# Experts' outputs as token rows, four of ten output groups held in PSUM, and h kept by rows only

## The reference

```python
def peer(x, w_q, sub_keys, u_tab, v_tab):
    ...
        q = jnp.einsum('td,dc->tc', xb, w_q).reshape(PEER_BLOCK, PEER_HEADS, 2, D_KEY // 2)
        s = jnp.einsum('thcd,hcnd->thcn', q, sub_keys, preferred_element_type=jnp.float32)
        ...
        sc, sel = lax.top_k(cand, PEER_TOPK)
        expert = jnp.take_along_axis(cid, sel, axis=-1)
        g = jax.nn.softmax(sc, axis=-1)
        a = jnp.einsum('td,thkd->thk', xb, u_tab[expert], preferred_element_type=jnp.float32)
        coef = (g * jax.nn.gelu(a, approximate=False)).astype(xb.dtype)
        return jnp.einsum('thk,thkd->td', coef, v_tab[expert])

def channel(h, norm_g, w_q, sub_keys, u_tab, v_tab):
    y = peer(rms_norm(h, norm_g).reshape(B * T, D), w_q, sub_keys, u_tab, v_tab)
    return h + y.reshape(B, T, D)
```

## Time and profile before

| | |
|---|---|
| median of three runs | 3685.9 us (3684.55 to 3686.02) |
| the profiled execution, first to last instruction | 3683.9 us |
| TensorE matmul busy | 3206.2 us, 87% |
| VectorE busy | 2776.0 us, 75% |
| ScalarE busy | 1194.5 us, 32% |
| GpSimd busy | 1217.5 us, 33% |

### The profile page before, as it was taken

One profiled execution on the slowest core, in us unless ns is written; L12 is line 12 of the kernel. 1 busy time (PEld: TensorE's weight loads), 2 busy tenths in 40 slices (PEclk: granted clock), 3 DMA queues, 4 the chain that ended last, 5 costly groups with the idle time before them and its releaser, 6 DMA issues. The chain is left out here.

```text
span 3683.9 us, 63681 instructions
## 1 busy us (share of the span) xinstructions
PE 3206.2 (87%) x22587; PEld 2843.2 (77%) x22587; DVE 2776.0 (75%) x6688; ACT 1194.5 (32%) x2269; POOL 1217.5 (33%) x1214
## 2 busy tenths in 40 slices
PE   7999588999367778647579999999999999999998
PEld 5777355666135556547479999999999999999998
DVE  6553455333124889899679999999999999999998
ACT  5443244444122322259622222222122122222221
POOL 0000122222120000000055565555655565555554
PEclk9999799999678888879889999999999999999999
DMA  4322789887676655307799999999999999999997
GB/s 146 117 66 73 254 275 335 274 297 240 240 265 208 205 194 212 120 26 220 214 365 356 330 343 349 330 348 354 332 344 341 344 348 337 342 348 327 348 342 274
DMA packets 405555, 993.05 MB, mean 270 GB/s; under 512 B 37938, under 2 KB 165908, under 8 KB 404052
## 3 DMA queue, kind: packets, MB, share of 16 engines
q0 software_dynamic: 150048, 595.57, 44.8%
q1 hardware_dynamic: 252932, 383.53, 30.2%
q10 hardware_dynamic: 2368, 11.54, 0.8%
HBM read 911.56 MB, written 146.44 MB: 287 GB/s over the span
## 5 line engine op out<-in xcount | busy, mean ns | idle before, releaser
L2118 PE MATMUL banks<-x_hi,u_hi 128*128 128x320 f32 x2048 | 634.1, 310 | 52.6 <-DVE x_lo L2207 52.6
L2131 PE MATMUL banks<-coef_hi,v_hi 128*128 128x320 f32 x2048 | 633.7, 309 | 6.9 <-issue 6.0
L2118 PE MATMUL banks<-x_lo,u_hi 128*128 128x320 f32 x2048 | 633.9, 310 | 0.0
L2118 PE MATMUL banks<-x_hi,u_lo 128*128 128x320 f32 x2048 | 633.8, 309 | 0.0
L2131 PE MATMUL banks<-coef_lo,v_hi 128*128 128x320 f32 x2048 | 633.5, 309 | 0.0
L2131 PE MATMUL banks<-coef_hi,v_lo 128*128 128x320 f32 x2048 | 633.4, 309 | 0.0
L2079 POOL DMA_INDIRECT uv_row<-in_v_rows,expert_tok x384 | 477.6, 1244 | 385.4 <-DVE y_tok L2261 335.1
L2079 POOL DMA_INDIRECT uv_row<-in_u_rows,expert_tok x384 | 462.9, 1205 | 347.7 <-DVE dots L2235 295.9
L2261 DVE SCALAR_TENSOR_TENSOR y_tok<-uv_row,share,y_tok 128x1024 f32<-128x1024 f32 x415 | 530.3, 1278 | 0.7
L2235 DVE CUSTOM_DVE_ANT_0 uv_row<-uv_row,x_tok 128x1024 f32<-128x1024 f32 x416 | 506.2, 1218 | 0.0
L2118 PEld LDWEIGHTS banks<-x_hi,u_hi 128*128 128x128 f32 x2048 | 385.3, 188 | 52.8 <-DVE x_lo L2207 52.8
(11 more groups left out here) (256 smaller groups left out, 5408.2 us busy)
## 6 DMA issues: line engine op xcount, KB each, us to landing
keys_ps<-in_cache_k SPq DMA_DIRECT2D x256, 256.0 KB, 4.8
values_ps<-in_cache_v POOLq DMA_DIRECT2D x256, 256.0 KB, 4.6
uv_raw<-in_u SPq DMA_DIRECT2D x128, 512.0 KB, 7.5
uv_raw<-in_v SPq DMA_DIRECT2D x128, 512.0 KB, 7.6
scratch_gates<-stage SPq DMA_DIRECT2D x10, 4096.0 KB, 23.6
gates<-scratch_gates SPq DMA_DIRECT2D x128, 320.0 KB, 6.4
out_win_k_out<-in_state_k POOLq DMA_DIRECT2D x8, 4088.0 KB, 15.1
out_win_v_out<-in_state_v POOLq DMA_DIRECT2D x8, 4088.0 KB, 26.5
```

Source lines behind the costliest of these rows:

```text
L2118: ins = nc.tensor.matmul(bank[:, 2 * r + c, 0:CH], u[r][a][:, k * P:(k + 1) * P], x2[b][:, k, c * CH:(c + 1) * CH], start=(k == 0 and a == b),
L2131: ins = nc.tensor.matmul(bank[:, 4 + n % 4, 0:CH], v[j][a][:, k * P:(k + 1) * P], coef[j][b][:, c * CH:(c + 1) * CH], start=(j == 0 and a ...
```

## The change

The outputs are computed with the operands swapped: a 128x128 slice of coef (128 experts by 128 tokens) is stationary and 512 columns of v move, so that the product is 128 tokens by 512 values. There are ten groups of 12 matmuls (5 token tiles by two halves of D) in place of sixteen. Groups 6 to 9 stay in banks 4 to 7 through all 32 turns and are added to y once, after the last. Groups 0 to 5 are added every turn as before, from two banks (2 and 3). The order on PE is 0, 6, 1, 7, 2, 8, 3, 9, 4, 5. The activations keep two banks (0 and 1). DVE does its 16 units of a y slot in lots of 2, 4, 4, 3, 3 and 0 ahead of the six adds. y lies by token rows in SBUF and is stored in five pieces of 512 KB; the first three wait for groups 1, 3 and 5, the last two for the held ones. h is kept by rows alone for all nine tiles: its transposes, their copies and the `hT` store are gone, and `run_experts` loads h from `h_rows`.

```diff
@@ mix_and_route
                 r = slice(T * P, T * P + P)
+                sp.wait_ge(h_ready, n + 1)
+                sp.dma_start(io["h_rows"][r, :], h[:, :]).then_inc(h_rows_stored, 16)
                 if dense[n]:
-                    sp.wait_ge(hT_ready, (dense_before(n) + 1) * 2)
-                    sp.dma_start(io["hT"][:, :, r].rearrange("k p t -> p k t"), hT[:, :, :]).then_inc(hT_stored, 16)
...
-                if dense[n]:
-                    for b in range(2):
-                        for j in range(4):
-                            ins = nc.tensor.transpose(bank[:, b, j * P:(j + 1) * P], h[:, (4 * b + j) * P:(4 * b + j + 1) * P], ident)
-                        ins.then_inc(hT_in_psum, 1)
                 pe.wait_ge(xr_ready, n + 1)
...
-                if dense[n]:
-                    since(act, hT_stored, dense_before(n) * 16)
-                    for b in range(2):
-                        act.wait_ge(hT_in_psum, dense_before(n) * 2 + b + 1)
-                        nc.scalar.copy(hT[:, 4 * b:4 * b + 4, :].rearrange("p k t -> p (k t)"), bank[:, b, :]).then_inc(hT_ready, 1)
...
-                if n:
-                    since(dve, hT_in_psum, dense_before(n) * 2)
-                    since(dve, h_rows_stored, rows_before(n) * 16)
+                since(dve, h_rows_stored, n * 16)
...
+OUTS_HELD = 4
+OUTS_ADDED = 2 * DT - OUTS_HELD
+Y_UNITS = 16
+BEFORE_ADDS = (2, 4, 4, 3, 3, 0)
...
+def output_order():
+
+    held, out = iter(range(OUTS_ADDED, 2 * DT)), []
+    for n in range(OUTS_ADDED):
+        out.append(n)
+        k = next(held, None)
+        if k is not None:
+            out.append(k)
+    return out
+
+
+def output_at(n):
+
+    return n // 2, slice(n % 2 * 512, (n % 2 + 1) * 512)
...
@@ run_experts
-        yT = sb("y_T", [P, KD, ND])
+        y = sb("y_dense", [P, DT, D])
+        x2_whole = y[:, :, :].rearrange("p q d -> p (q d)").rearrange("p (k t) -> p k t", k=KD)
...
-        AN, YN = TC, KD * TC
+        y_held, y_held_added = sems("y_held_done"), sems("y_held_added")
+        AN, YN = TC, OUTS_ADDED
...
-            sp.dma_start(yT[:, :, :], io["hT"][:, :, 0:ND].rearrange("k p t -> p k t")).then_inc(h_loaded, 16)
+            sp.dma_start(y[:, :, :], io["h_rows"][0:ND, :].rearrange("(q p) d -> p q d", p=P)).then_inc(h_loaded, 16)
...
-            for k in range(KD):
-                sp.wait_ge(y_added, SUPER * YN - (KD - 1 - k) * TC)
-                sp.dma_start(io["yT"][k, :, :], yT[:, k, :]).then_inc(y_stored, 16)
+            for q in range(DT):
+                if 2 * q < OUTS_ADDED:
+                    sp.wait_ge(y_added, (SUPER - 1) * YN + 2 * q + 2)
+                else:
+                    sp.wait_ge(y_held_added, 2 * q + 2 - OUTS_ADDED)
+                sp.dma_start(io["y_rows"][q * P:(q + 1) * P, :], y[:, q, :]).then_inc(y_stored, 16)
...
-                    since(pe, gelu_done, i * AN + (c - 3))
+                    since(pe, gelu_done, i * AN + (c - 1))
...
-                            ins = nc.tensor.matmul(bank[:, 2 * r + c, 0:CH], u[r][a][:, k * P:(k + 1) * P],
+                            ins = nc.tensor.matmul(bank[:, c, 0:CH], u[r][a][:, k * P:(k + 1) * P],
...
-                for n in range(YN):
-                    k, c = n // TC, n % TC
-                    since(pe, y_added, s * YN + (n - 3))
+                first, last = isinstance(s, int) and s == 0, isinstance(s, int) and s == SUPER - 1
+                for n in output_order():
+                    q, cols = output_at(n)
+                    held = n >= OUTS_ADDED
+                    to = bank[:, 4 + n - OUTS_ADDED if held else 2 + n % 2, :]
+                    if not held:
+                        since(pe, y_added, s * YN + (n - 1))
                     for j in range(BLK):
                         for a, b in ((0, 0), (0, 1), (1, 0)):
-                            ins = nc.tensor.matmul(bank[:, 4 + n % 4, 0:CH], v[j][a][:, k * P:(k + 1) * P],
-                                                   coef[j][b][:, c * CH:(c + 1) * CH], start=(j == 0 and a == b),
-                                                   stop=(j == BLK - 1 and a == 1))
-                    ins.then_inc(y_in_psum, 1)
+                            ins = nc.tensor.matmul(to, coef[j][a][:, q * P:(q + 1) * P], v[j][b][:, cols],
+                                                   start=(j == 0 and a == b and (first or not held)),
+                                                   stop=(j == BLK - 1 and a == 1 and (last or not held)))
+                    if not held:
+                        ins.then_inc(y_in_psum, 1)
+                    elif last:
+                        ins.then_inc(y_held, 1)
...
-                nc.vector.tensor_tensor(out, out, bank[:, 4 + n % 4, 0:CH], ALU.add).then_inc(y_added, 1)
+                nc.vector.tensor_tensor(out, out, bank[:, 2 + n % 2, :], ALU.add).then_inc(y_added, 1)
+
+            def add_held(n):
+                dve.wait_ge(y_held, n - OUTS_ADDED + 1)
+                q, cols = output_at(n)
+                out = y[:, q, cols]
+                nc.vector.tensor_tensor(out, out, bank[:, 4 + n - OUTS_ADDED, :], ALU.add).then_inc(y_held_added, 1)
...
-                    for n in range(YN):
-                        add(i, n)
-                        if n < len(in_slot[slot]):
-                            unit(in_slot[slot][n])
+                    todo = iter(in_slot[slot])
+                    for n in output_order():
+                        if n < OUTS_ADDED:
+                            for k in range(BEFORE_ADDS[n]):
+                                here = next(todo, None)
+                                if here is not None:
+                                    unit(here)
+                            add(i, n)
+                        elif i == SUPER - 1:
+                            add_held(n)
```

More of the change, by code:

```diff
@@ L1356, in mix_and_route @@
         hrstd = sb("h_rstd4", [P, 1])
-        hT = sb("h_T", [P, KD, P])
         xr = sb("h_scaled", [P, D])
@@ L1417, in mix_and_route @@
         picks_in_psum, picksT_ready = sem("picks_in_psum"), sem("picksT_ready")
-        hT_stored, x2T_stored = sem("hT_stored"), sem("x2T_stored")
+        x2T_stored = sem("x2T_stored")
         h_rows_stored, xg_stored = sem("h_rows_stored"), sem("xg_stored")
@@ L1469, in _ @@
                 sp.wait_ge(picks_stored, 32)
-            sp.wait_ge(hT_stored, 16 * dense_before(N))
             sp.wait_ge(x2T_stored, 16 * dense_before(N))
-            sp.wait_ge(h_rows_stored, 16 * rows_before(N))
+            sp.wait_ge(h_rows_stored, 16 * N)
             sp.wait_ge(xg_stored, 16 * (rows_before(N) + (PACK - 1 if tiles[-1] == TILES - 1 else 0)))
@@ L1926, in units_of_slots @@
     for slot in slots():
-        n = 0 if slot == ("a", 0) else 2 + slot[1] % 2 if slot[0] == "a" else KD * TC
+        n = 0 if slot == ("a", 0) else 2 + slot[1] % 2 if slot[0] == "a" else Y_UNITS
         n = min(n, len(row_units()) - taken)
@@ L2025, in load_x2 @@
                 some = slice(part * X2_PART, (part + 1) * X2_PART)
-                sp.dma_start(yT[:, some, :], io["x2T"][some, :, 0:ND].rearrange("k p t -> p k t")).then_inc(x2_loaded[part], 16)
+                sp.dma_start(x2_whole[:, some, :], io["x2T"][some, :, 0:ND].rearrange("k p t -> p k t")).then_inc(x2_loaded[part], 16)
             load_raw(0)
@@ L2055, in _ @@
                         load_raw(n)
-            for k in range(KD):
-                sp.wait_ge(y_added, SUPER * YN - (KD - 1 - k) * TC)
-                sp.dma_start(io["yT"][k, :, :], yT[:, k, :]).then_inc(y_stored, 16)
+            for q in range(DT):
[4 more added lines that the diff above has]
+                sp.dma_start(io["y_rows"][q * P:(q + 1) * P, :], y[:, q, :]).then_inc(y_stored, 16)
             sp.wait_ge(y_s_ready, 2)
             sp.dma_start(io["y_s"], h_s).then_inc(y_stored, 16)
-            sp.wait_ge(y_stored, 16 * (KD + 1))
+            sp.wait_ge(y_stored, 16 * (DT + 1))
         @block.gpsimd
@@ L2072, in store_y @@
             def store_y(q):
-                pool.dma_start(io["y_rows"][q * P:(q + 1) * P, :], y_tok[q % 2][:, :]).then_inc(y_rows_stored, 16)
+                pool.dma_start(io["y_rows"][(DT + q) * P:(DT + q + 1) * P, :], y_tok[q % 2][:, :]).then_inc(y_rows_stored, 16)
             def fetch(n):
@@ L2185, in _ @@
                 act.wait_ge(x2_loaded[k // X2_PART], 16)
-                nc.scalar.copy(x2[0][:, k, :], yT[:, k, :]).then_inc(x2_hi, 1)
+                nc.scalar.copy(x2[0][:, k, :], x2_whole[:, k, :]).then_inc(x2_hi, 1)
             act.wait_ge(x2_lo, KD)
@@ L2200, in _ @@
                         act.wait_ge(a_in_psum, i * AN + (c + 1))
-                        nc.scalar.activation(w[i % 2][:, c * CH:(c + 1) * CH], bank[:, 2 * (i % 2) + c, 0:CH], ACT.Gelu).then_inc(gelu_done, 1)
+                        nc.scalar.activation(w[i % 2][:, c * CH:(c + 1) * CH], bank[:, c, 0:CH], ACT.Gelu).then_inc(gelu_done, 1)
         @block.vector
@@ L2274, in add @@
```

(16 more changed lines are left out.)

6 lines of the change are left out of this document (removed).

## The result

The changed kernel takes 3652.2 us (median of four runs; 3650.7 to 3657.2) against 3685.8 us (four runs; 3684.6 to 3686.0) for the kernel before. The ratio is 0.991, with an interval of 0.9897 to 0.9924. The profiled execution of the changed kernel has a span of 3651.1 us, that of the kernel before 3683.9.

The account below looks back on a forecast made before the run. The prediction took PE's issue of matmuls as the bound, with DVE and DMA close behind. Terms of -30.5 + 0.5 + 2 - 0.5 = -28.5 us on 3683.9 gave 3655.4, plus 2.0 for the median: 3657.4 us, range 3650 to 3668.

## What to carry to other kernels

Where PE's issue sets the pace, count its matmuls as well as its columns: find rows of two sizes in the same trace, take the columns off, and what is left, 13 ns here, is what each matmul saved by a wider shape is worth. Read it at the sizes between which you change, since at 128 columns the rows here give another. Keeping sums in PSUM over many turns pays only if the engine that adds is the bound; here it took DVE from 0.945 to 0.905 of the time and gave nothing, and it moved work to the end, where it showed as 2.0 to 3.3 us. A buffer that must be given back within 3.5 us rather than 10.6 costs nothing while its releaser has slack; measure the slack by making the releaser late on purpose, and count instructions in a window, since short stalls of PE don't appear among the waits.

## What the runs showed of the hardware

A matmul of this type, each with its own load of a 128x128 stationary, starts every 0.1197 us at 256 columns, 0.1466 at 320 and 0.2267 at 512, all at the 2.4 GHz level: the columns' time and 13.0 to 13.4 ns. It holds with the DMA engines at a share of 0.93 to 0.95, whichever operand is stationary. Stalls of PE of some 0.1 us leave its busy time at 1199.5 of 1200 us while 42 of 6785 matmuls, 6.2 us, are missing from it. A store of 128 KB on SP's queue landed in 4.0 us behind three stores of 512 KB that left together, in 2.6 behind two and in 1.9 to 2.0 behind one. An add of 128x512 from PSUM takes 687 ns on DVE.
